# Layer 1's query-key scores of a hybrid encoder: three passes of rounded halves in two row tiles in place of native float32 products

## The chip, the cores and the metric

The kernel runs on one NeuronCore of one Trainium2 chip, as one launch. The metric is the device time of an execution in microseconds (us). The engines are TensorE (PE: matmuls; PEld: its weight loads, which overlap them), VectorE (DVE), ScalarE (ACT), GpSimdE (POOL) and SyncE (SP), each working through its own instructions in order and waiting on semaphores for the others.

## The reference

Two layers of a bidirectional encoder on x of 512 tokens by 1024 channels, all in float32. What a layer does, and of it the part that the change touches:

```python
h = modulate(rms_norm(x, norm1_g[l]), sh1, sc1)
z = h @ w_in[l]                      # split into za, zb, zq, zk, zv
# attention: 4 heads, 2 components of 64 dimensions each, 128 queries at a time
q = apply_rope(rms_norm(q, q_g), cos, sin) * (QK_HEAD_DIM ** -0.5)
k = apply_rope(rms_norm(k, k_g), cos, sin)
s = jnp.einsum("bqhcd,bkhcd->bhcqk", qb, k)
p = jax.nn.softmax(s, axis=-1)
w = p[:, :, 0] - lam * p[:, :, 1]
o = jnp.einsum("bhqk,bkhe->bqhe", w, v)
# beside it a 31-tap convolution and a gated 3-tap convolution, all three normed
x = x + g1 * (concat(ya, yb, yc) @ w_out[l])
x = x + g2 * swiglu(modulate(rms_norm(x, norm2_g[l]), sh2, sc2))
```

## The kernel before

Channels lie on the 128 partitions and the 512 tokens along the free axis. Every large product is made of three passes in the type float32r, which is float32 rounded to fewer bits: for each operand a rounded half ("hi") and a remainder ("lo") are kept, and hi·hi, hi·lo and lo·hi are summed in PSUM. `product` (L1294 to L1299) is one such triple for a chunk of 128 channels and 512 tokens. The weights arrive as a stream of units of 128 x 1024; ScalarE writes each unit's rounded half (`split_hi`, L539) and VectorE the remainder (`split_lo`, L842), into rings of four.

A layer runs as units on TensorE: the input projection for convolution and keys, for queries (four units), for values (four), then six units of the short convolution (the B units, `b_part`, each in four parts), which are dealt out among the attention's tiles; then W_out, the gate and up product and the down product.

After the projection the keys and queries are normed and rotated on VectorE (`qk_rotate`, L1021 to L1035) into `qk`, with tokens on the partitions. TensorE transposes them head by head: the keys (L1444) into PSUM banks 0 to 3, one bank for a head, ScalarE copies these to `k_t` (`copy_k_t`, L608), and then the queries (L1453) into the same four banks, once the copy of the key that lies there is done; ScalarE copies them to `q_t` (`copy_q_t`, L612). These copies hold 128 partitions: the first component of a head on partitions 0 to 63, the second on 64 to 127.

There are 16 attention tiles, a head by 128 queries each. For a tile TensorE makes `scores` (L1486), two native float32 products, one for each component, on 64 rows of the array each (two row tiles), into a pair of banks. VectorE takes the row maximum (`row_max`, L1040), ScalarE the two exponentials with their sums (`exps`, L621), VectorE the reciprocals (`row_inverse`, L1047), ScalarE scales the first component (`scale_p0`, L630), VectorE mixes in the second (`row_mix_in`, L1055), TensorE transposes the result (`weights_t`, L1499), ScalarE copies it out (`copy_w_t`, L639), and `attend` (L1511) multiplies by the values.

The order on each engine is written out by hand. On TensorE, tile `it` is: a part of a B unit, an attend step of an earlier head, `scores(it + 2)`, another part of the B unit, `weights_t(it)`. `scores(0)` and `scores(1)` stand behind the transposes of the queries and the B part 0, and B parts 1 to 3 behind them. On ScalarE: `copy_w_t(it - 1)`, `scale_p0(it)`, `exps(it + 1)`, then what else the tile has. On VectorE, between `qk_rotate` and the first `row_max` stand the remainders of three weight units and eight taps of the 31-tap convolution (`conv_a_taps`, L959), and in the tiles, behind `row_max(it + 1)` and `row_mix_in(it)`, more taps, the short convolution and a unit's remainder in every second tile. The buffers of the mixer lie over those of the feed-forward part; behind the mixer's there is a spare region of 16 KB a partition.

Of the kernel before, what the change touches and what calls it, by code (L numbers as in the profile page):

```python
# [7 lines left out]
F32 = mybir.dt.float32  # L8
F32R = mybir.dt.float32r
I32 = mybir.dt.int32  # L10
ALU = mybir.AluOpType
ACT = mybir.ActivationFunctionType
AX_X = mybir.AxisListType.X

P = 128
D = 1024
T = 512
# [9 lines left out]
HEADS = 4  # L27
DV = 128
DQ = 64
# [118 lines left out]
def encoder_kernel(nc, x_in, c_in, pos_in, freq_in, pcol_in, rows_in, ada_in, w_in, out):  # L148
    ctx = ExitStack()
    with ctx:  # L150
        top = [nc.sbuf_base]

        def place(name, shape, dt=F32, at=None):

            size = 4 * int(np.prod(shape[1:]))
            size += -size % 32
            if at is None:
                at = top[0]
                top[0] += size
            return nc.alloc_sbuf_tensor_at(name, shape, dt, offset=at), at + size  # L160
# [4 lines left out]
        def sem(name):  # L165
            return ctx.enter_context(nc.semaphore(name))
# [48 lines left out]
        at = gu_base  # L215
        ua, at = place("ua", [P, CC, T + 2 * PAD_A], at=at)
        uc, at = place("uc", [P, CC, T], at=at)
        hb, at = place("hb", [P, CC, T + 2 * PAD_B], at=at)
        yb, at = place("yb", [P, CC, T], at=at)
        rope_base = at  # L220
        tn, at = place("tn", [P, 2, T], at=at)
        tb, at = place("tb", [P, 2, T], at=at)
        ta, at = place("ta", [P, 2, T], at=at)
        prob, _ = place("prob", [P, PROBS, 2, T], at=rope_base)
        qk_base = at
        qk, at = place("qk", [P, 2, NT, T], at=at)
        w_t = [place(f"w_t{i}", [P, NT, T], at=qk_base + 4 * NT * T * i)[0] for i in range(2)]
        v, at = place("v", [P, NT, T], at=at)
        qt_base = at
        q_t, at = place("q_t", [P, HEADS, T], at=at)  # L230
        k_t, at = place("k_t", [P, HEADS, T], at=at)
        oc0, _ = place("oc0", [P, T], at=sq_base)
        oc1, at = place("oc1", [P, T], at=at)
        oc = [oc0, oc1]
        spare_base = at
        at += 4 * 4 * D
        c_row, _ = place("c_row", [1, D], at=spare_base)
        lam_prod, at = place("lam_prod", [P, 2 * L, DQ], at=at)
        assert at <= gu_end, "the mixer's buffers fit gu"


        sq0, _ = place("sq_first", [P, KC, T], at=h_lo_base)
        turns, at = place("turns", [P, NT, HALF, len(TERMS)], at=rope_base)
        whole, at = place("whole_turns", [P, NT, HALF, len(TERMS)], at=at)
        ang, at = place("ang", [P, 5, NT, HALF], at=at)
        ang_hi, at = place("ang_hi", [P, NT, HALF], F32R, at=at)
        assert at <= qk_base
        first_ring, at = place("ada_ring_first", [P, 8, D], at=qk_base)
        assert at <= qt_base + 4 * HEADS * T
        mid_a, _ = place("ada_ring_mid_a", [P, 4, D], at=spare_base)  # L250
        mid_b, _ = place("ada_ring_mid_b", [P, 4, D], at=qt_base)
        gu_ring, at = place("ada_ring_gu", [P, 4, D], at=gu_end - 4 * 4 * D)
        assert at <= gu_end and 4 * 4 * D == 4 * T * (FC - 2 * GU_MOD_STEPS)
        late_ring, at = place("ada_ring_late", [P, 8, D], at=h_base)
# [12 lines left out]
        ps = ctx.enter_context(nc.psum_tensor("ps", [P, 8, T], F32))  # L267
# [80 lines left out]
        s_qt = sem("q_t_ready")  # L348
        s_kt = sem("k_t_ready")

        s_scores = sem("scores_ready")
        s_max = sem("max_ready")
        s_exp = sem("exp_ready")
# [181 lines left out]
        def _(act):  # L535
# [69 lines left out]

            def copy_k_t(l, h):
                act.wait_ge(s_ktr, HEADS * l + h + 1)
                act.activation(k_t[:, h, :], ps[:, h, :], ACT.Copy).then_inc(s_kt, 1)  # L608

            def copy_q_t(l, h):  # L610
                act.wait_ge(s_qtr, HEADS * l + h + 1)
                act.activation(q_t[:, h, :], ps[:, h, :], ACT.Copy).then_inc(s_qt, 1)  # L612

            def exps(l, it):
                I = N_TILES * l + it
# [97 lines left out]
            for l in range(L):  # L713
# [45 lines left out]
                for h in range(HEADS):  # L759
                    copy_k_t(l, h)  # L760
# [75 lines left out]
        def _(dve):  # L836
# [172 lines left out]
            def qk_rotate(l, X, t):  # L1009
# [24 lines left out]
                dve.wait_ge(s_rot, 2 * E + 2)  # L1034
                dve.tensor_tensor(qk[:, X, t], ta[:, e % 2], tb[:, e % 2], ALU.add).then_inc(s_rope, 1)  # L1035

            def row_max(l, it):
                dve.wait_ge(s_scores, N_TILES * l + it + 1)
                b = 2 * (it % 2)
                dve.tensor_reduce(neg_max[:, it, :], ps[:, b:b + 2, :], AX_X, ALU.max,  # L1040
                                  negate=True).then_inc(s_max, 1)

            def row_inverse(l, it):

                I = N_TILES * l + it
                dve.wait_ge(s_exp, 2 * I + 2)
                dve.reciprocal(row_inv[:, it, :], row_sum[:, it, :]).then_inc(s_inv, 1)  # L1047
# [57 lines left out]
            for l in range(L):  # L1105
# [20 lines left out]
                for s in range(first, U_B):  # L1126
# [36 lines left out]
                    if l == 0 and s == U_V + 2:  # L1163
# [6 lines left out]
                                              ALU.mult).then_inc(s_lam, 1)  # L1170
                        dve.wait_ge(s_lam, 2 * L)

                row_max(l, 0)
                row_inverse(l, 0)
                for it in range(N_TILES):
# [110 lines left out]
        def _(pe):  # L1286
# [19 lines left out]
            h, gu = (h_hi, h_lo), (gu_hi, gu_lo)  # L1306
# [46 lines left out]
            def token_chunk(u, n, t, bank):  # L1353

                r = n % 2
                hs = [p[:, n, t * P:(t + 1) * P] for p in h]
                ws = [w[:, u % RING, r * T:(r + 1) * T] for w in (w_hi, w_lo)]
                pe.matmul(ps[:, bank, :], hs[0], ws[0], start=n == 0, stop=False)  # L1358
                pe.matmul(ps[:, bank, :], hs[0], ws[1], start=False, stop=False)  # L1359
                return pe.matmul(ps[:, bank, :], hs[1], ws[0], start=False, stop=n == KC - 1)  # L1360
# [30 lines left out]
            for b in range(2):  # L1391
                mm = pe.matmul(ps[:, b, :], ones[0:1, :], c_row[:, b * T:(b + 1) * T], start=True, stop=True)
            mm.then_inc(s_cps, 1)
            warm_up(N_WARM)
            for k in range(0, KC, 2):
                pe.wait_ge(s_pair, k // 2 + 1)
                mm = pe.matmul(ps[:, B_STAT, :], ones[:], sq0[:, k, :], start=k == 0, stop=k == KC - 2)
# [3 lines left out]
            for l in range(L):  # L1401
# [11 lines left out]
                for kk in range(N_Q):  # L1413
                    u = U + U_Q + kk
                    weights_split(u)
                    for t in range(NT):
# [6 lines left out]
                        for n in (2 * kk, 2 * kk + 1):  # L1423
                            mm = token_chunk(u, n, t, B_Q[t])
                    mm.then_inc(s_unit, 1)

                for kk in range(N_V):
                    u = U + U_V + kk
                    weights_split(u)
                    for t in range(NT):  # L1430
# [3 lines left out]
                        for n in (2 * kk, 2 * kk + 1):  # L1434
                            mm = token_chunk(u, n, t, B_KV[t])
# [13 lines left out]
                for hd in range(HEADS):  # L1449

                    pe.wait_ge(s_kt, HEADS * l + hd + 1)
                    for tt in range(NT):
                        tr = pe.transpose(ps[:, hd, tt * P:(tt + 1) * P], qk[:, 1, tt, hd * P:(hd + 1) * P], ident[:])  # L1453
                    tr.then_inc(s_qtr, 1)
# [20 lines left out]
                def scores(it):  # L1475
                    hd, qt = divmod(it, NT)
                    if it < 2:

                        pe.wait_ge(s_qt, HEADS * l + 2 * it + 2)
                        pe.wait_ge(s_kt, HEADS * (l + 1))  # L1480
                    else:

                        pe.wait_ge(s_exp, 2 * (N_TILES * l + it - 1))
                    for comp in range(2):
                        r = slice(DQ * comp, DQ * (comp + 1))
                        mm = pe.matmul(ps[:, 2 * (it % 2) + comp, :], q_t[r, hd, qt * P:(qt + 1) * P],  # L1486
                                       k_t[r, hd, :], start=True, stop=True)
                    mm.then_inc(s_scores, 1)
# [36 lines left out]
                for it in range(N_TILES):  # L1525
                    if 0 < it < 2 * N_B - 1:
                        b_part(2 * it + 2)
                    hd, kt = divmod(it - NT - 1, NT)
# [42 lines left out]
                with pe.Fori(0, 2) as i:  # L1571
                    for c in range(4):
# [3 lines left out]
                        for j, nb in enumerate(DOWN_BLOCKS):  # L1576
                            pe.wait_ge(s_gu, FC * l + f + nb)
                            unit(U + U_DOWN + 3 * c + j, B_DOWN + c % 2, gu, range(f, f + nb), i, 12,
                                 start=j == 0, stop=j == len(DOWN_BLOCKS) - 1)
# [83 lines left out]
```

## Time and profile before

| what | value |
|---|---|
| median of 3 runs | 1229.51 us (1228.2 to 1231.56) |
| the profiled execution's own time | 1227.94 us |
| its span, first to last instruction | 1226.1 us |
| mean granted TensorE clock, share of full speed | 0.986 |
| PE busy | 1185.7 us, 97% of the span |
| PE weight loads | 926.8 us, 76% |
| VectorE busy | 717.6 us, 59% |
| ScalarE busy | 481.1 us, 39% |
| GpSimdE busy | 104.5 us, 9% |
| layer 1's attention tiles | about 724 to 811 us of the span |

Matmuls are pipelined: a row's duration holds the way through the array, and the distance from one start to the next is what a matmul costs in a stream. A group of rows of one kind is merged into one line with its count.

### The profile page before, as it was taken

How to read it: one execution, taken by the hardware profiler on the slowest of the kernel's cores; microseconds unless marked ns; L12 is line 12 of the kernel's file. 1: busy time of each engine (PE TensorE's matmuls, PEld its weight loads, DVE VectorE, ACT ScalarE, POOL GpSimd, SP SyncE). 2: the span in 40 equal slices, each digit the busy share in tenths (PEclk: the TensorE clock that was granted, in tenths of full speed). 3: DMA queues.
4: the chain of work that ended last, by engine and by line, in shares of the span. 5: the costliest groups of instructions: out<-in, count | busy, mean ns of one | idle time of the engine just before them, and what ended most of it. 6: DMA issues, size and time to landing. Idle time of an engine off the chain costs nothing.

```text
span 1226.1 us, 14230 instructions
## 1 busy us (share of the span) xinstructions
PE 1185.7 (97%) x5090; PEld 926.8 (76%) x5090; DVE 717.6 (59%) x1022; ACT 481.1 (39%) x720; POOL 104.5 (9%) x177
## 2 busy tenths in 40 slices
PE   8999998979999999999989999889899999999998
PEld 5887545858888888888868876457788888888887
DVE  7889987876556433466656999746633333333331
ACT  5555777342332322322242356764422322322220
POOL 2411323101012000111000001100000000000000
PEclk9999999989999999999989999999999999999999
DMA  8686445646565232677313221103132232233322
GB/s 312 242 235 156 88 106 201 227 152 223 188 202 186 91 103 93 267 248 248 137 68 104 86 69 52 52 1 121 69 103 97 92 103 92 96 103 104 103 103 86
DMA packets 46345, 165.71 MB, mean 135 GB/s; under 512 B 5409, under 2 KB 5537, under 8 KB 46306
## 3 DMA queue, kind: packets, MB, share of 16 engines
q1 hardware_dynamic: 30386, 107.13, 25.9%
q0 software_dynamic: 15920, 58.07, 15.3%
q8 instruction: 23, 0.38, 0.1%
q14 instruction: 16, 0.13, 0.0%
HBM read 163.09 MB, written 2.10 MB: 135 GB/s over the span
## 4 chain that ended last, share of the span: by engine, by line
PE 78%; DVE 13%; ACT 3%; issue 3%; DMA 2%; SPq 0%; POOL 0%; DVEq 0%; ACTq 0%
PE ps L1297 21%; PE ps L1299 21%; PE ps L1298 21%; PE ps L1327 3%; DVE uc L959 2%; DVE w_lo L842 2%; PE ps L1511 2%; PE ps L1486 2%; PE ps L1331 2%; PE ps L1386 1%; DMA ada_ring_first<-ada 1%; DMA raw<-w_stream 1%; ACT prob L621 1%; DVE tn L1021 1%; DVE neg_max L1040 1%
## 5 line engine op out<-in xcount | busy, mean ns | idle before, releaser
L539 ACT ACTIVATE w_hi<-raw 128x1024 fp32r<-128x1024 f32 x196 | 207.8, 1060 | 570.6 <-PE ps L1299 494.7
L842 DVE TENSOR_TENSOR w_lo<-raw,w_hi 128x1024 fp32r<-128x1024 f32 x182 | 223.3, 1227 | 266.1 <-ACT w_hi L539 265.8
L1297 PE MATMUL ps<-h_hi,w_hi 128*128 128x512 f32 x848 | 334.5, 394 | 0.0
L1299 PE MATMUL ps<-h_lo,w_hi 128*128 128x512 f32 x848 | 330.4, 390 | 0.0
L1298 PE MATMUL ps<-h_hi,w_lo 128*128 128x512 f32 x848 | 330.2, 389 | 0.0
L1297 PEld LDWEIGHTS ps<-h_hi,w_hi 128*128 128x128 f32 x848 | 159.2, 188 | 48.3 <-issue 16.7
L1299 PEld LDWEIGHTS ps<-h_lo,w_hi 128*128 128x128 f32 x848 | 159.2, 188 | 33.2
L1298 PEld LDWEIGHTS ps<-h_hi,w_lo 128*128 128x128 f32 x848 | 159.3, 188 | 31.8
L1297 PE MATMUL ps<-gu_hi,w_hi 128*128 128x512 f32 x352 | 136.9, 389 | 0.0
L1298 PE MATMUL ps<-gu_hi,w_lo 128*128 128x512 f32 x352 | 136.9, 389 | 0.0
L1299 PE MATMUL ps<-gu_lo,w_hi 128*128 128x512 f32 x352 | 136.9, 389 | 0.0
L1245 DVE TENSOR_TENSOR work_b<-ps,work_a 128x512 f32<-128x512 f32 x44 | 30.4, 691 | 115.8 <-PE ps L1299 92.4
L959 DVE SCALAR_TENSOR_TENSOR uc<-ua,pcol,uc 128x512 f32<-128x512 f32 x120 | 83.9, 743 | 0.0
L1297 PEld LDWEIGHTS ps<-gu_hi,w_hi 128*128 128x128 f32 x352 | 66.1, 188 | 13.8
L1299 PEld LDWEIGHTS ps<-gu_lo,w_hi 128*128 128x128 f32 x352 | 66.1, 188 | 13.7
L1298 PEld LDWEIGHTS ps<-gu_hi,w_lo 128*128 128x128 f32 x352 | 66.1, 188 | 13.6
L1358 PE MATMUL ps<-w_hi,h_hi 128*128 128x512 f32 x192 | 75.1, 391 | 0.1
L1360 PE MATMUL ps<-w_hi,h_lo 128*128 128x512 f32 x192 | 74.7, 389 | 0.0
L1359 PE MATMUL ps<-w_lo,h_hi 128*128 128x512 f32 x192 | 74.7, 389 | 0.0
L621 ACT ACTIVATE prob<-ps,neg_max 128x512 f32<-128x512 f32 x64 | 43.5, 685 | 34.9 <-DVE neg_max L1040 34.9
L1089 DVE SCALAR_TENSOR_TENSOR xT<-ps,mod,xT 128x512 f32<-128x512 f32 x32 | 24.0, 750 | 52.9 <-PE ps L1299 50.4
L444 POOL TENSOR_SCALAR row_mix<-row_inv,neg_lam 128x1 f32<-128x1 f32 x32 | 26.3, 823 | 223.1 <-DVE row_inv L1047 223.1
(171 smaller groups left out, 1301.0 us busy)
## 6 DMA issues: line engine op xcount, KB each, us to landing
raw<-w_stream SPq DMA_DIRECT2D x196, 512.0 KB, 3.3
ada_ring_gu<-ada POOLq DMA_DIRECT2D x28, 512.0 KB, 4.1
ada_ring_late<-ada POOLq DMA_DIRECT2D x28, 512.0 KB, 4.7
ada_ring_first<-ada POOLq DMA_DIRECT2D x16, 512.0 KB, 5.4
w_lo<-w_stream POOLq DMA_DIRECT2D x14, 512.0 KB, 7.7
ada_ring_mid_a<-ada POOLq DMA_DIRECT2D x12, 512.0 KB, 6.2
ada_ring_mid_b<-ada POOLq DMA_DIRECT2D x12, 512.0 KB, 4.6
xT<-x_t SPq DMA_DIRECT2D x4, 512.0 KB, 5.6
```

The source lines that it names most:

```text
L539: act.activation(w_hi[:, u % RING, :], raw[:, u % RAW, :], ACT.Copy).then_inc(s_whi, 1)
L621: act.activation(prob[:, it % PROBS, comp, :], ps[:, 2 * (it % 2) + comp, :], ACT.Exp, bias=neg_max[:, it, comp:comp + 1], accum_out=row_s ...
L842: dve.tensor_tensor(w_lo[:, u % RING, :], raw[:, u % RAW, :], w_hi[:, u % RING, :].bitcast(F32), ALU.subtract).then_inc(s_wlo, 1)
L959: dve.scalar_tensor_tensor(uc[:, c, :], ua[:, c, j:j + T], w, uc[:, c, :], ALU.mult, ALU.add).then_inc(s_tap, 1)
L1245: dve.tensor_tensor(wb[:, f, :], ps[:, j, :], wa[:, f, :], ALU.mult).then_inc(s_pr, 1)
L1297: pe.matmul(dst, whi, rhs[0][:, n, :], start=start, stop=False)
L1298: pe.matmul(dst, wlo, rhs[0][:, n, :], start=False, stop=False)
L1299: return pe.matmul(dst, whi, rhs[1][:, n, :], start=False, stop=stop)
L1327: pe.matmul(ps[:, bank, :], wp[:, u % RING, n * P:(n + 1) * P], h_hi[:, n, :], start=b == 0 and wp is w_hi, stop=False)
L1358: pe.matmul(ps[:, bank, :], hs[0], ws[0], start=n == 0, stop=False)
L1359: pe.matmul(ps[:, bank, :], hs[0], ws[1], start=False, stop=False)
L1360: return pe.matmul(ps[:, bank, :], hs[1], ws[0], start=False, stop=n == KC - 1)
```

## The change

In layer 1 alone, the copies of the transposed keys and queries are written as float32r (rounded) into the places where `k_t` and `q_t` lay. VectorE gets eight new subtractions, four `k_low` and four `q_low`, which read the transposed head from its PSUM bank, subtract the rounded copy, and write the remainder to two new buffers in the spare region. They stand in VectorE's order between the last tap ahead of the tiles and the first `row_max`. On TensorE the transposes of query head `hd` wait for `k_low(hd)` too, since they overwrite the bank that it reads, and `scores(0)` and `scores(1)` wait for the remainders. `scores` in layer 1 is six float32r matmuls of 64 rows by 512 columns, the two components taking turns: hi·hi, lo·hi, hi·lo of each. Layer 0 keeps its native products.

```diff
--- before.py
+++ after.py
@@ -229,12 +229,16 @@
         qt_base = at
         q_t, at = place("q_t", [P, HEADS, T], at=at)
         k_t, at = place("k_t", [P, HEADS, T], at=at)
+        q_r, _ = place("q_t_hi", [P, HEADS, T], F32R, at=qt_base)
+        k_r, _ = place("k_t_hi", [P, HEADS, T], F32R, at=qt_base + 4 * HEADS * T)
         oc0, _ = place("oc0", [P, T], at=sq_base)
         oc1, at = place("oc1", [P, T], at=at)
         oc = [oc0, oc1]
         spare_base = at
         at += 4 * 4 * D
         c_row, _ = place("c_row", [1, D], at=spare_base)
+        q_lo, k_lo_at = place("q_t_lo", [P, HEADS, T], F32R, at=spare_base)
+        k_lo, _ = place("k_t_lo", [P, HEADS, T], F32R, at=k_lo_at)
         lam_prod, at = place("lam_prod", [P, 2 * L, DQ], at=at)
         assert at <= gu_end, "the mixer's buffers fit gu"
 
@@ -348,6 +352,8 @@
         s_qt = sem("q_t_ready")
         s_kt = sem("k_t_ready")
 
+        s_klo = sem("k_t_lo_ready")
+        s_qlo = sem("q_t_lo_ready")
         s_scores = sem("scores_ready")
         s_max = sem("max_ready")
         s_exp = sem("exp_ready")
@@ -605,11 +611,11 @@
 
             def copy_k_t(l, h):
                 act.wait_ge(s_ktr, HEADS * l + h + 1)
-                act.activation(k_t[:, h, :], ps[:, h, :], ACT.Copy).then_inc(s_kt, 1)
+                act.activation((k_r if l else k_t)[:, h, :], ps[:, h, :], ACT.Copy).then_inc(s_kt, 1)
 
             def copy_q_t(l, h):
                 act.wait_ge(s_qtr, HEADS * l + h + 1)
-                act.activation(q_t[:, h, :], ps[:, h, :], ACT.Copy).then_inc(s_qt, 1)
+                act.activation((q_r if l else q_t)[:, h, :], ps[:, h, :], ACT.Copy).then_inc(s_qt, 1)
 
             def exps(l, it):
                 I = N_TILES * l + it
@@ -1033,6 +1039,18 @@
                 dve.wait_ge(s_cos, E + 1)
                 dve.wait_ge(s_rot, 2 * E + 2)
                 dve.tensor_tensor(qk[:, X, t], ta[:, e % 2], tb[:, e % 2], ALU.add).then_inc(s_rope, 1)
+
+            def k_low(h):
+
+                dve.wait_ge(s_kt, HEADS + h + 1)
+                dve.tensor_tensor(k_lo[:, h, :], ps[:, h, :], k_r[:, h, :].bitcast(F32),
+                                  ALU.subtract).then_inc(s_klo, 1)
+
+            def q_low(h):
+
+                dve.wait_ge(s_qt, HEADS + h + 1)
+                dve.tensor_tensor(q_lo[:, h, :], ps[:, h, :], q_r[:, h, :].bitcast(F32),
+                                  ALU.subtract).then_inc(s_qlo, 1)
 
             def row_max(l, it):
                 dve.wait_ge(s_scores, N_TILES * l + it + 1)
@@ -1170,6 +1188,11 @@
                                               ALU.mult).then_inc(s_lam, 1)
                         dve.wait_ge(s_lam, 2 * L)
 
+                if l:
+                    for h in range(HEADS):
+                        k_low(h)
+                    for h in range(HEADS):
+                        q_low(h)
                 row_max(l, 0)
                 row_inverse(l, 0)
                 for it in range(N_TILES):
@@ -1449,6 +1472,8 @@
                 for hd in range(HEADS):
 
                     pe.wait_ge(s_kt, HEADS * l + hd + 1)
+                    if l:
+                        pe.wait_ge(s_klo, hd + 1)
                     for tt in range(NT):
                         tr = pe.transpose(ps[:, hd, tt * P:(tt + 1) * P], qk[:, 1, tt, hd * P:(hd + 1) * P], ident[:])
                     tr.then_inc(s_qtr, 1)
@@ -1478,9 +1503,21 @@
 
                         pe.wait_ge(s_qt, HEADS * l + 2 * it + 2)
                         pe.wait_ge(s_kt, HEADS * (l + 1))
+                        if l:
+                            pe.wait_ge(s_klo, HEADS)
+                            pe.wait_ge(s_qlo, 2 * it + 2)
                     else:
 
                         pe.wait_ge(s_exp, 2 * (N_TILES * l + it - 1))
+                    if l:
+                        cols = slice(qt * P, (qt + 1) * P)
+                        for i, (q, k) in enumerate(((q_r, k_r), (q_lo, k_r), (q_r, k_lo))):
+                            for comp in range(2):
+                                r = slice(DQ * comp, DQ * (comp + 1))
+                                mm = pe.matmul(ps[:, 2 * (it % 2) + comp, :], q[r, hd, cols], k[r, hd, :],
+                                               start=i == 0, stop=i == 2)
+                        mm.then_inc(s_scores, 1)
+                        return
                     for comp in range(2):
                         r = slice(DQ * comp, DQ * (comp + 1))
                         mm = pe.matmul(ps[:, 2 * (it % 2) + comp, :], q_t[r, hd, qt * P:(qt + 1) * P],
```

## Rows read from the trace of the kernel before

**Rows 1.** Window: length, PE, PEld, DVE, ACT, POOL busy us; granted clock; DMA.

```profile
740.00:780.00 40.00, 39.99 (x167) 24.32 (x167) 36.95 (x56) 27.09 (x58) 5.01 (x8) 1.00 0.17 59
```

**Rows 2.** Timeline of PE at the tiles' start: start, length, engine, line, operation.

```profile
720.56 1.91 PE L1453 MATMUL ps<-ident,qk 128*128 128x128 f32 x16
722.22 0.48 PE L1297 MATMUL ps<-h_hi,w_hi 128*128 128x512 f32 x1
...
723.79 1.99 PE L1486 MATMUL ps<-k_t,q_t 64*128 64x512 f32 x8
725.71 0.50 PE L1297 MATMUL ps<-h_hi,w_hi 128*128 128x512 f32 x1
```

**Rows 3.** Timeline of DVE in the same stretch.

```profile
724.22 1.41 DVE L959 SCALAR_TENSOR_TENSOR uc<-ua,pcol,uc 128x512 f32<-128x512 f32 x2
725.55 1.22 DVE L1040 TENSOR_REDUCE neg_max<-ps 128x2 f32<-128x1024 f32 x1
728.29 0.17 DVE L1047 RECIPROCAL row_inv<-row_sum 128x2 f32<-128x2 f32 x1 [1.51 <-ACT prob L621]
```

**Rows 4.** Timeline of DVE: a 128x512 two-operand step out of PSUM, and its successor.

```profile
745.51 0.68 DVE L967 TENSOR_TENSOR hb<-ps,yb 128x512 f32<-128x512 f32 x1
746.11 1.21 DVE L842 TENSOR_TENSOR w_lo<-raw,w_hi 128x1024 fp32r<-128x1024 f32 x1
```

**Rows 5.** Timeline of ACT: the four copies of the queries.

```profile
722.20 2.05 ACT L612 ACTIVATE q_t<-ps 128x512 f32<-128x512 f32 x4
```

**Rows 6.** Timeline of PE about scores(4).

```profile
736.95 0.39 PE L1298 MATMUL ps<-h_hi,w_lo 128*128 128x512 f32 x1
737.17 0.40 PE L1299 MATMUL ps<-h_lo,w_hi 128*128 128x512 f32 x1
737.50 1.13 PE L1486 MATMUL ps<-k_t,q_t 64*128 64x512 f32 x4
738.56 0.50 PE L1297 MATMUL ps<-h_hi,w_hi 128*128 128x512 f32 x1
738.89 0.39 PE L1298 MATMUL ps<-h_hi,w_lo 128*128 128x512 f32 x1
```

**Rows 7.** Line L1486 alone at scores(4): durations min/median/max, first and last start.

```profile
L1486 PEld LDWEIGHTS ps<-k_t,q_t x4: 183/184/186, 737.5 to 737.6; 64*128 64x128 f32 x4
L1486 PE MATMUL ps<-k_t,q_t x4: 589/641/693, 737.5 to 738.0; 64*128 64x512 f32 x4
```

**Rows 8.** Timeline: the mixes and transposes of tiles 4 and 10, and copy and scaling behind.

```profile
748.38 0.74 DVE L1055 SCALAR_TENSOR_TENSOR prob<-prob,row_mix 128x512 f32<-128x512 f32 x1
749.17 0.66 PE L1499 MATMUL ps<-ident,prob 128*128 128x128 f32 x4
...
782.17 0.60 PE L1499 MATMUL ps<-ident,prob 128*128 128x128 f32 x4
782.81 0.60 ACT L639 ACTIVATE w_t<-ps 128x512 f32<-128x512 f32 x1 [1.73 <-PE ps L1499]
784.05 0.75 DVE L1055 SCALAR_TENSOR_TENSOR prob<-prob,row_mix 128x512 f32<-128x512 f32 x1 [1.62 <-ACT prob L630]
```

**Rows 9.** Timeline of PE: what follows an idle stretch in layer 1's tiles.

```profile
790.44 1.04 PE L1499 MATMUL ps<-ident,prob 128*128 128x128 f32 x4 [3.01 <-DVE prob L1055]
```

**Rows 10.** Windows, columns as in the first group: behind two idle stretches of PE.

```profile
793.00:794.00 1.00, 1.00 (x3) 0.54 (x2) 0.00 (x0) 1.00 (x3) 0.00 (x0) 0.51 0.00 0
794.00:795.00 1.00, 1.00 (x3) 0.44 (x3) 0.04 (x1) 1.00 (x3) 0.00 (x0) 1.00 0.00 0
...
633.00:634.00 1.00, 1.00 (x4) 0.78 (x4) 1.00 (x2) 0.27 (x2) 0.00 (x0) 0.72 0.00 0
```

**Rows 11.** Timeline of PE at the start of layer 1, behind an idle stretch.

```profile
627.94 0.77 PE L1343 MATMUL ps<-h_hi,w_hi 128*128 128x512 f32 x1 [3.13 <-ACT h_hi L577]
628.50 0.63 PE L1344 MATMUL ps<-h_hi,w_lo 128*128 128x512 f32 x1
628.93 0.63 PE L1343 MATMUL ps<-h_hi,w_hi 128*128 128x512 f32 x1
```

## The prediction

> **What bounds the kernel now.** I read the windows first. In layer 1's tiles from 740 to 780 us TensorE is busy for 39.99 of 40 us and VectorE for 36.95, at full granted clock [rows 1]: both are nearly full, and the change takes work from the one and gives work to the other. So the question is which of them sets the pace where. Next I read the timelines at the start of the tiles. TensorE goes from the key and query transposes through the B part 0 and the first two scores to the next B part, from 720.56 to 725.71, with no idle entry [rows 2]. VectorE works off its last taps (724.22) and takes the first row maximum at 725.55, the moment it gets to it [rows 3]; the scores were there by then. Until tile 10 TensorE lags a little behind VectorE. For tile 4 the weights are mixed at 748.38 + 0.74 = 749.12 and the transposes start at 749.17, so here the two meet. For tile 10 it is TensorE that is late: its transposes start at 782.17, ScalarE had waited 1.73 us for them, and VectorE 1.62 us for ScalarE [rows 8]. From there to W_out the chain runs through VectorE and ScalarE; a delay that reaches it reaches the end, because W_out, gate and up and down are a closed stream of TensorE.
>
> **The saving in scores, per tile.** A float32r matmul in a stream costs 0.22 to 0.23 us from start to start (736.95 to 737.17). The native scores(4) run from 737.50 to 738.56, 1.06 us, and the matmul behind is followed by the next at 0.33 instead of 0.23, as is the one ahead of scores: a switch costs some 0.1 us on either side, and I leave it as it is [rows 6]. The line's own view gives four matmuls with two starts, 737.5 and 738.0: the two components run at the same time in the two row tiles, in two rounds of some 0.47 us, with 0.12 left over [rows 7]. The change makes it three rounds of one float32r pass. If the two row tiles run together as the native ones do, a round is 0.23 us at the least and, with the 0.04 that the native round has over its 0.43 (two passes of 0.213), 0.27 at the most; I take 0.25. Then scores cost 3 x 0.25 + 0.12 = 0.87, a saving of 0.19 us; the bounds are 0.81 and 0.93, a saving of 0.25 or 0.13. I round up to 0.2 a tile since the switch may shrink with the type unchanged. Sixteen tiles would be 3.2 us, but only a part of them counts, as follows.
>
> **The new wait, which is the larger term.** `k_low(0)` stands behind the taps in VectorE's order, so it can't start before 725.55 [rows 3], though the key's transposes and copies were done about 7 us earlier. The query transposes, at 720.56 before [rows 2], wait for it. What is queued behind that wait on TensorE: the B part 0, the scores, all tiles. A `k_low` is a two-operand step of 128x512 out of PSUM: 0.68 us, 0.60 from start to start [rows 4]. So `k_low` 0 to 3 end at 726.24, 726.84, 727.45 and 728.05, and TensorE, its values done by about 720.6, idles for some 5.5 us.
>
> After idle stretches the clock was low. Behind 3.01 us of idle the four transposes at 790.44 took 1.04 instead of 0.60 us [rows 8, 9], and the granted clock was about half until 794.0 [rows 10], 3.6 us after work resumed. Behind 3.13 us at the start of layer 1, matmuls came 0.43 us apart instead of 0.23 [rows 11], and the clock was back only in the 633 to 634 window, 5.6 us after the work resumed [rows 10]. Both levels are those of 1.2 and 2.4 GHz. An idle of 5.5 us will do the same, so I take the low clock for the transposes and the B part 0. The Trainium skill, "TensorE: Matmul & The Clock Gate", section "HAM oscillation — how this bites in real kernels", warns of exactly such gaps between bursts; the trace agrees, with the two stretches above.
>
> The chain then: a head's four transposes take 4 x 0.213 = 0.85 at the low clock (the 1.04 less the way out of the array), so from 726.3 four heads end at 729.7. ScalarE copies at 0.5 to 0.6 each [rows 5], the last done at 730.5; `q_low` 0 to 3 end at about 728.8, 729.5, 730.3 and 731.2. The B part 0, six matmuls, takes 6 x 0.43 = 2.6 instead of about 1.5, so it ends at 732.3. scores(0), waiting on `q_low(1)` only, run from 732.35 to 733.2, and the row maximum can start at about 733.25 instead of 725.55: **VectorE is 7.7 us late.** Bounds: if the clock is back after 3.6 us, 1.0 us less (6.7); if it stays low through scores(0) too, 0.8 more (8.5); if it never falls, the transposes follow `k_low` to 728.55, the B part ends at 730.05, the row maximum starts at 731.2: 5.65 late. The eight subtractions themselves (8 x 0.60 = 4.8 us of VectorE) lie inside this delay.
>
> **What is given back.** scores(1) end about 0.85 us behind scores(0), so TensorE comes to the B part 1 about 8.1 us late (725.71 before). It gains 0.2 a tile and meets VectorE again at tile 4, where there was no slack; from there VectorE's 7.7 is what counts. Of the scores behind that, 7 to 12 are ahead of the transposes of tile 10: 6 x 0.2 = 1.2 us, all of it within the 1.73 us that ScalarE waited there [rows 8]. So 1.2 us comes back, 1.7 at most. Scores 13 to 15 have slack, and save nothing. VectorE's other short waits in the tiles are on ScalarE, which is delayed with it, so I let them give nothing back; if they did, they hold 40 - 36.95 = 3 us in the 40 us [rows 1].
>
> **The rest at no cost.** The copies in float32r are the same size on the same engine; the remainders of weight units move with VectorE, and the rings are two units ahead; no DMA is moved or added.
>
> **Sum.** 7.7 - 1.2 = 6.5 us on the profiled execution's 1227.94: 1234.4. The median of the runs shown is 1229.51, 1.57 above the profiled one; on the median the forecast is **1236.0 us**. Bounds of this case: 5.0 (6.7 - 1.7) to 8.0 (8.5 with little given back), 1234.5 to 1237.5.
>
> **Rivals.**
> 1. *Not slower than can be measured: the clock stays up or the delay is soaked up.* Were TensorE not slowed after the gap, VectorE would be 5.65 late, and 1.2 to 1.7 would come back: 4.0 to 4.5. If in addition VectorE's waits in the tiles (3 us) give back 1 us or more, the sum is about 3: 1232.5. Against it: two of two rows behind gaps of 3 us show the low clock. It decides from a delay under 3.7 us. Chance 0.15.
> 2. *The two row tiles do not run together in float32r.* Then scores cost 6 x 0.227 + 0.12 = 1.48, 0.42 more a tile than native, and TensorE, not VectorE, is behind throughout. scores(0) make the delay 8.3, scores(1) another 1.0, scores 2 to 12 eleven times 0.42 = 4.6, so tile 10's transposes are 13.9 late: about 1243.4. For it: no row shows float32r in row tiles; against it: native ones run in pairs [rows 7]. Chance 0.08.
> 3. *They run together, but a row tile's next weight load is not hidden under its own matmul.* Transposes of 128 columns follow each other at about 0.11 us (four from 782.17, the last ending at 782.77 [rows 8]), which I take as the bound of a load: a round 0.23 + 0.11 = 0.34, scores 1.13, 0.07 more than native. The delay is 8.0, TensorE another 0.7, plus 11 x 0.07 = 0.8: 9.4, or 1238.9. Chance 0.10. The Trainium skill ("TensorE: Matmul & The Clock Gate", section "The mechanism" of its part on packing) says that loads overlap matmuls in flight only where the row group differs, which would speak for this rival; the loads of scores(4) start at 737.5 and 737.6, the second pair while the first pair's matmuls run on the same rows [rows 7], which speaks against it.
> 4. *Faster.* It would need the query transposes not to wait for the taps; the order on VectorE is fixed, and the saving in scores, 0.25 x 16 = 4 us at the very best, is under even the shortest delay. Chance 0.02.
>
> **How the numbers follow.** The forecast's case has 0.65. The range of 80% takes in its bounds, rival 3 and the upper part of rival 1: 1232.0 to 1240.0 us; rival 2, the faster case and the lower part of rival 1 are left out. About 0.3% (3.7 us) is what a measurement of this kernel can tell from no change. Faster by more: 0.02. Within: rival 1 and a little of the forecast's case where more is given back, 0.17. Slower: 0.81.
>
> **What would show it.** In the profile after: an idle of about 5.5 us ahead of the query transposes, released by `k_low` on VectorE; granted clock 0.5 behind it for 3 to 6 us; the first row maximum about 7.7 us later against the start of the query transposes of before; scores from start to the next matmul 0.87 us with pairs of starts; the wait of ScalarE for tile 10's transposes shrunk from 1.73 to about 0.5. I am wrong if the gap is there and the first row maximum is less than 5.5 us late, if scores cost over 1.06, or if the distance from the first row maximum to the first W_out matmul shrinks by more than 2 us.

## The result, and the profile after

The changed kernel takes 1234.25 us (median of 13 runs, 1232.68 to 1235.7), the kernel before 1227.94 us beside it (13 runs, 1224.82 to 1231.56): a ratio of 1.0054, with a 95% interval of 1.0044 to 1.0063. That is 6.6 us slower (5.4 to 7.7). The two medians by themselves differ by 6.3 us: here and below, the us by which a kernel is slower or faster are the ratio applied to the time of the kernel before, and the difference of the medians is up to 1.1 us away from that. The forecast was 6.5 us slower; its absolute figure, 1236.0, is 1.75 us too high, mostly because the first three runs of the kernel before, on which it stood, had a median of 1229.51, 1.57 above that of all 13.

The spans of the two profiled executions differ by 5.7 us (1231.8 against 1226.1), but the key transposes of layer 1 start at 712.64 us after and at 716.02 before, although nothing ahead of them was changed. So the stretches are measured from that start. "To tile 13's row maximum" begins at the first row maximum, and "to first W_out matmul" at tile 13's. Three profiles of each kernel, all in us:

| | key transposes to first row maximum | to tile 13's row maximum | to first W_out matmul | sum |
|---|---|---|---|---|
| before, three profiles | 9.53, 9.53, 9.53 | 62.96, 62.94, 62.96 | 17.79, 18.99, 18.36 | 90.28, 91.46, 90.85 |
| after, three profiles | 17.42, 16.02, 16.97 | 61.91, 61.89, 61.87 | 18.97, 18.11, 18.71 | 98.30, 96.02, 97.55 |

The means of the sums are 90.9 and 97.3: 6.4 us, inside the measured 5.4 to 7.7. The first stretch loses 7.3 us on the mean, the second gives back 1.06, and the third is 0.2 longer on the mean (18.38 and 18.60), while it moves by up to 1.2 us between executions of one kernel. From the first W_out matmul to the end of the span it takes 419.8, 420.9 and 420.7 us before and 420.9, 420.5 and 420.8 after, which adds 0.3.

The gap, in TensorE's timeline after (start, length, engine, line, operation, count, and in brackets the idle time ahead and who ended it):

```profile
716.94 0.39 PE L1383 MATMUL ps<-w_hi,h_lo 128*128 128x512 f32 x1
723.00 3.64 PE L1478 MATMUL ps<-ident,qk 128*128 128x128 f32 x16 [5.68 <-DVE k_t_lo L1046]
726.30 0.78 PE L1320 MATMUL ps<-h_hi,w_hi 128*128 128x512 f32 x1
726.87 0.63 PE L1321 MATMUL ps<-h_hi,w_lo 128*128 128x512 f32 x1
727.30 0.63 PE L1322 MATMUL ps<-h_lo,w_hi 128*128 128x512 f32 x1
```

TensorE idles 5.68 us ahead of the query transposes, which follow the last value product at once in [rows 2]. The 16 transposes take 3.64 us for 1.91 there, and the B part's matmuls stand 0.43 us apart. VectorE in the same stretch:

```profile
720.85 1.41 DVE L965 SCALAR_TENSOR_TENSOR uc<-ua,pcol,uc 128x512 f32<-128x512 f32 x2
722.18 2.47 DVE L1046 TENSOR_TENSOR k_t_lo<-ps,k_t_hi 128x512 fp32r<-128x512 f32 x4
724.76 0.69 DVE L1052 TENSOR_TENSOR q_t_lo<-ps,q_t_hi 128x512 fp32r<-128x512 f32 x1
727.32 0.69 DVE L1052 TENSOR_TENSOR q_t_lo<-ps,q_t_hi 128x512 fp32r<-128x512 f32 x1 [0.16 <-ACT q_t_hi L618]
730.06 1.23 DVE L1058 TENSOR_REDUCE neg_max<-ps 128x2 f32<-128x1024 f32 x1 [2.06 <-PE ps L1517]
```

Where the first row maximum stood behind the last taps in [rows 3], now the four key subtractions stand, and the row maximum waits another 2.06 us for the scores. Four windows of this stretch (length, busy time of PE, PEld, DVE, ACT and POOL, granted clock, DMA share, GB/s):

```profile
721.00:722.00 1.00, 0.00 (x0) 0.00 (x0) 1.00 (x2) 0.00 (x0) 0.00 (x0) 1.00 0.00 0
723.00:724.00 1.00, 1.00 (x5) 1.00 (x6) 1.00 (x3) 0.00 (x0) 0.00 (x0) 0.50 0.63 254
727.00:728.00 1.00, 1.00 (x4) 0.81 (x3) 0.84 (x2) 0.28 (x1) 0.00 (x0) 0.50 0.00 0
729.00:730.00 1.00, 1.00 (x9) 0.81 (x10) 0.00 (x0) 0.00 (x0) 0.00 (x0) 1.00 0.00 0
```

VectorE is busy alone, then the granted clock is half (1.2 GHz) until the 729 window. The new scores, and the transposes of tile 10 with what they release, answering to [rows 6] and [rows 8]:

```profile
742.11 0.50 PE L1517 MATMUL ps<-k_t_hi,q_t_hi 64*128 64x512 f32 x2
742.45 0.39 PE L1517 MATMUL ps<-k_t_hi,q_t_lo 64*128 64x512 f32 x2
742.68 0.40 PE L1517 MATMUL ps<-k_t_lo,q_t_hi 64*128 64x512 f32 x2
743.01 0.50 PE L1320 MATMUL ps<-h_hi,w_hi 128*128 128x512 f32 x1
...
785.62 0.60 PE L1536 MATMUL ps<-ident,prob 128*128 128x128 f32 x4
786.26 0.60 ACT L645 ACTIVATE w_t<-ps 128x512 f32<-128x512 f32 x1 [0.72 <-PE ps L1536]
787.50 0.75 DVE L1073 SCALAR_TENSOR_TENSOR prob<-prob,row_mix 128x512 f32<-128x512 f32 x1 [0.56 <-ACT prob L636]
```

Three pairs of starts, and 0.90 us from the first to the next matmul, for 1.06 before. ScalarE waits 0.72 us for the transposes of tile 10, for 1.73, and VectorE 0.56 for 1.62: that is the 1.06 us given back (1.62 - 0.56).

### The profile page after: what moved, and what is told of

It is laid out like the page before. It is cut to its first block, busy times and chain, and to the rows that moved or that the text cites. A ratio compares the mean times of both kernels' runs of the same rounds, so it can differ in the third digit from the quotient of the medians.

```text
span 1231.8 us, 14307 instructions
## 1 busy us (share of the span) xinstructions
PE 1185.9 (96%) x5122; PEld 932.8 (76%) x5122; DVE 722.4 (59%) x1030; ACT 481.4 (39%) x720; POOL 105.4 (9%) x177
## 4 chain that ended last, share of the span: by engine, by line
PE 80%; DVE 13%; ACT 4%; issue 3%; DMA 0%; DVEq 0%; ACTq 0%
PE ps L1320 21%; PE ps L1322 21%; PE ps L1321 21%; PE ps L1350 3%; DVE uc L965 3%; DVE w_lo L848 2%; PE ps L1548 2%; PE ps L1354 2%; DVE neg_max L1058 1%; ACT prob L627 1%; PE ps L1366 1%; PE ps L1367 1%; PE ps L1371 1%; PE ps L1381 1%; PE ps L1383 1%
```

## The experiments

Each ratio is against the kernel before, with its 95% interval. "Sum" is the way from the key transposes to the first W_out matmul in the experiment's profile (before 90.3 to 91.5, after 96.0 to 98.3).

**The wait without the passes.** Layer 1's scores stay native and read unrounded copies; the remainders are made and not used.

```diff
-                    if l:
-                        cols = slice(qt * P, (qt + 1) * P)
-                        for i, (q, k) in enumerate(((q_r, k_r), (q_lo, k_r), (q_r, k_lo))):
...
-                        return
```

> The eight subtractions and all their waits as in the changed kernel, but layer 1's scores stay native float32 (from unrounded copies; the remainders are computed and not used). My theory (the early wait costs, the passes give a little back): the idle of some 5.7 us ahead of the query transposes and the low clock behind it stay, the first row maximum is about 8 us late, and what the changed kernel got back at tile 10 (ScalarE's wait there went from 1.73 to 0.72 us) is not given back: 1 to 1.2 us slower than the changed kernel, so some 7.5 to 8 us over the kernel before, a ratio of 1.0062. Rival (the passes themselves are what costs, by row tiles or accumulation): this kernel is clearly faster than the changed one, ratio under 1.003.

Measured: 1.0062 (1.0046 to 1.0078), 7.6 us over the kernel before; sum 98.5 with only 3.4 us of low clock in the gap. ScalarE at tile 10, and VectorE behind it:

```profile
787.14 0.60 ACT L645 ACTIVATE w_t<-ps 128x512 f32<-128x512 f32 x1 [1.73 <-PE ps L1527]
788.38 0.75 DVE L1073 SCALAR_TENSOR_TENSOR prob<-prob,row_mix 128x512 f32<-128x512 f32 x1 [2.02 <-ACT prob L636]
```

Nothing is given back: the wait of 1.73 us is that of [rows 8]. From the first to tile 13's row maximum it takes 63.35 us for 61.91, so the passes save the changed kernel 1.44 us here. That is 0.4 more than they save against the kernel before, since VectorE's wait at tile 10 is 2.02 us here for 1.62 there; where these 0.4 come from is open. The subtractions and their waits hold the whole loss, as my theory has it; the rival that the passes cost something falls. That this kernel is slower than the changed one is shown by the stretch, not by the two ratios, whose intervals overlap.

**The passes without the wait.** Three passes of the rounded halves, without subtractions and their waits.

```diff
-                        for i, (q, k) in enumerate(((q_r, k_r), (q_lo, k_r), (q_r, k_lo))):
+                        for i, (q, k) in enumerate(((q_r, k_r), (q_r, k_r), (q_r, k_r))):
```

> Three float32r passes in the two row tiles as in the changed kernel, but all three take the rounded halves, and there are no subtractions and no waits for them. It leaves out the remainders, so the scores are three times the rounded product. My theory: 0.16 us less a tile on TensorE (scores 0.90 instead of 1.06), of which only what ScalarE waited for TensorE at tile 10 counts: 1.0 to 1.7 us faster than the kernel before, ratio 0.9988. Rival (TensorE sets the pace throughout, so all 16 tiles count): 2.6 us faster, 0.9979. Rival (float32r in row tiles costs): slower than before.

Measured: 0.9974 (0.9963 to 0.9986), 3.2 us faster (1.7 to 4.5), more than the 1.0 to 1.7 expected. ScalarE at tile 10:

```profile
779.25 0.60 ACT L645 ACTIVATE w_t<-ps 128x512 f32<-128x512 f32 x1 [0.72 <-PE ps L1526]
```

The same 0.72 as after, and 61.89 us from the first row maximum to tile 13's: 1.07 saved, as the theory has it. The time by itself speaks for the first rival: its 0.9979 lies inside the interval, and the theory's 0.9988 just outside. The stretch speaks against it, since the twelve scores in it at 0.16 us each would save 1.9 us if TensorE set the pace in all tiles. The sum is 89.3, 1.6 below the mean of before, and the way from W_out to the end is 419.9 us, 0.6 below; together 2.1 us, inside the measured 1.7 to 4.5. So the tiles answer as expected, and the half of these 2.1 us that lies behind tile 13 is of the size by which executions of one kernel differ there. Whether the passes have a part in it stays open.

**The gap filled.** 24 matmuls of 128x512 into a bank that is overwritten later, between the values and the query transposes.

```diff
+                if l:
+                    weights_split(U + U_B)
+                    pe.wait_ge(s_v, NT * l + 1)
+                    for i in range(24):
+                        pe.matmul(ps[:, B_KV[0], :], w_hi[:, (U + U_B) % RING, 0:P], h_hi[:, i % KC, :],
+                                  start=True, stop=True)
```

> The changed kernel with 24 matmuls of 128x512 float32r, whose results are overwritten later, between the last value product and the query transposes: they fill the idle 5.7 us (24 x 0.227 = 5.45) and end just before the transposes may start. If the low clock behind the gap costs 2.2 us, as the accounting says (first row maximum 7.9 us late against 5.65 with the clock up), the first row maximum comes about 2.2 us earlier and the kernel is 2 us faster than the changed one: ratio 1.0036. If the clock plays no part (all is VectorE's order), the time is that of the changed kernel, 1.0054.

Measured: 1.0024 (1.0015 to 1.0034), 2.9 us over the kernel before. TensorE and VectorE at the gap:

```profile
718.83 5.60 PE L1476 MATMUL ps<-h_hi,w_hi 128*128 128x512 f32 x24
724.68 2.42 PE L1484 MATMUL ps<-ident,qk 128*128 128x128 f32 x16 [0.24 <-DVE k_t_lo L1046]
726.86 0.48 PE L1320 MATMUL ps<-h_hi,w_hi 128*128 128x512 f32 x1
...
729.45 1.22 DVE L1058 TENSOR_REDUCE neg_max<-ps 128x2 f32<-128x1024 f32 x1 [0.73 <-PE ps L1523]
```

The transposes start when `k_low` lets them, 0.24 us behind the filler, and take 2.42 us for 3.64; the granted clock is 1.00 in all windows from 633 to 792 us. The first row maximum is 15.14 us behind the key transposes, 5.61 late; the forecast's bound for a clock that stays up was 5.65. So the low clock is a real part of the delay: 1.7 us (7.3 - 5.6) of the 7.3 that the three profiles after have on the mean. The rival, by which the time would be the changed kernel's 1.0054, falls. The loss in time is 2.9 us for the changed kernel's 6.6, so 3.7 us less, more than this; the sum (95.7) is only 1.6 below the changed kernel's mean, and where the rest went was not found.

**The subtractions earlier in VectorE's order.** Same work, other place.

```diff
+                    if l and s == U_V + 1:
+                        for h in range(HEADS):
+                            k_low(h)
+                    if l and s == U_V + 2:
+                        for h in range(HEADS):
+                            q_low(h)
                     if s in TAPS_UNIT[l]:
                         conv_a_taps(l, TAPS_UNIT[l][s])
```

> The changed kernel with the four key subtractions moved ahead of the last eight taps, and the four query subtractions behind the first two of them and one weight unit's remainder, ahead of the last six taps. Same work. My theory: the wait of the query transposes goes (no idle ahead of them, clock stays up there), and scores(0) start about as before; but the last taps now stand between the subtractions and the first row maximum, which is 4.8 us late (8 x 0.60), and TensorE idles about 3 us ahead of scores(2) instead. With 1 us back at tile 10: 4 us slower than the kernel before, ratio 1.0033, 2.5 us faster than the changed one. Rival (the cost is the subtractions' own length and not their place in the order): no different from the changed kernel, 1.0054.

Measured: 1.0033 (1.002 to 1.0046), 4.1 us over the kernel before, 2.5 less than the changed one; sum 95.2. VectorE:

```profile
717.48 2.48 DVE L1046 TENSOR_TENSOR k_t_lo<-ps,k_t_hi 128x512 fp32r<-128x512 f32 x4
...
722.33 2.48 DVE L1052 TENSOR_TENSOR q_t_lo<-ps,q_t_hi 128x512 fp32r<-128x512 f32 x4
724.72 2.73 DVE L965 SCALAR_TENSOR_TENSOR uc<-ua,pcol,uc 128x512 f32<-128x512 f32 x4
727.37 1.22 DVE L848 TENSOR_TENSOR w_lo<-raw,w_hi 128x1024 fp32r<-128x1024 f32 x1
728.51 1.41 DVE L965 SCALAR_TENSOR_TENSOR uc<-ua,pcol,uc 128x512 f32<-128x512 f32 x2
729.84 1.21 DVE L1058 TENSOR_REDUCE neg_max<-ps 128x2 f32<-128x1024 f32 x1
```

The first row maximum is 4.80 us late, which is the eight subtractions at 0.60 and nothing else. TensorE's idle moved: 0.42 and 0.23 us ahead of the first two scores, 2.37 ahead of the third, and here the clock stayed up until tile 12 (1.00 in the windows from 729 to 738). The rival's 1.0054 is outside the interval. Place alone is worth some 2.5 us (the intervals of the two kernels just touch, but the first stretch takes 14.33 us for 16.02 to 17.42), and the work still costs.

**VectorE's order rewritten around them.** The first row maximum right behind the query subtractions, three taps in VectorE's wait for the first exponentials, three taps and a remainder later, and the remainder of tile 11 moved as in the next experiment.

```diff
-13: 2, 14: 4, 15: 2})
+13: 2, 14: 3})
...
+                        for h in range(HEADS):
+                            q_low(h)
+                        row_max(l, 0)
...
+                    if it == 13:
+                        split_lo(U + U_B + N_B - 1 + RING)
```

> The changed kernel's computation with VectorE's order rewritten in layer 1: key subtractions ahead of the last eight taps, query subtractions behind two of them and one weight unit's remainder, the first row maximum right behind them, three taps while ScalarE makes the first exponentials, the remainder of the next weight unit at the end of tile 0, three taps later (tiles 9, 10 and 12), and the remainder of tile 11 moved behind the row maximum of tile 13's turn. My theory (place in VectorE's order was the cost; the 4.8 us of subtractions are paid only where VectorE has no idle time): first row maximum within 0.5 us of before, 1.5 us of the subtractions go into the wait for the first exponentials, 2 to 2.6 us stay in the tiles, 1 to 1.6 us come back at tile 11, 1.1 us by the moved remainder: within 0.5 us of the kernel before, ratio 1.000 (0.999 to 1.001). Rival (VectorE's work is paid in full wherever it stands): 4.8 - 1.1 - 1.1 = 2.6 us slower, 1.002.

Measured: 1.0001 (0.999 to 1.0011), as my theory has it; the rival's 1.002 is outside, but see the next experiment, which changes what the rival would give. The first row maximum is 0.28 us earlier than before, the stretch to tile 13's takes 63.28 us (1.37 over after, with five taps of 0.66 us more in it), the sum is 90.3:

```profile
724.74 1.22 DVE L1058 TENSOR_REDUCE neg_max<-ps 128x2 f32<-128x1024 f32 x1
725.88 2.06 DVE L965 SCALAR_TENSOR_TENSOR uc<-ua,pcol,uc 128x512 f32<-128x512 f32 x3
727.86 0.16 DVE L1065 RECIPROCAL row_inv<-row_sum 128x2 f32<-128x2 f32 x1
```

The wait of 1.51 us ahead of the first reciprocals [rows 3] is gone, filled with taps. TensorE behind tile 12 here, and a window:

```profile
789.95 1.09 PE L1546 MATMUL ps<-ident,prob 128*128 128x128 f32 x4 [2.37 <-DVE prob L1073]
...
790.00:791.00 1.00, 1.00 (x4) 0.63 (x4) 0.75 (x3) 1.00 (x5) 0.00 (x0) 0.51 0.00 0
```

So here the clock fell behind an idle of 2.37 us, the length behind which it stayed up in the experiment before. The passes can be had at the time of the kernel before. But part of this edit, the moved remainder, has nothing to do with the passes, and what it gives has to be taken off.

**One remainder moved in the kernel before.** The last part of that edit alone, on the kernel before. The lines stand in the loop of both layers, but in layer 0 VectorE does not write this remainder (a DMA does), so only layer 1 changes.

```diff
                     if it + 1 < N_TILES:
                         row_max(l, it + 1)
+                    if it == 13:
+                        split_lo(U + U_B + N_B - 1 + RING)
                     row_mix_in(l, it)
...
-                    if it % 2 and it < 2 * N_B:
+                    if it % 2 and it < 2 * N_B - 1:
```

> The kernel before, with one thing moved in VectorE's order in layer 1: the remainder of the weight unit at tile 11 (1.13 us, ahead of the row maximum of tile 13, for which ScalarE waits 2.43 us) goes behind the row maximum of tile 14, where VectorE idles for 2.37 us. If the stretch behind tile 10 hangs on VectorE and ScalarE, as I take it, 1.1 us faster than before, ratio 0.9991; if on TensorE, no change.

Measured: 0.9977 (0.9966 to 0.9988), 2.8 us faster (the medians, 1224.44 and 1227.76, differ by 3.3), and faster than both kernels. The stretch to tile 13's row maximum is 1.13 us shorter (61.83), as expected. TensorE behind tile 12, and a window there:

```profile
786.11 0.66 PE L1501 MATMUL ps<-ident,prob 128*128 128x128 f32 x4 [1.88 <-DVE prob L1055]
...
787.00:788.00 1.00, 0.43 (x1) 0.30 (x2) 1.00 (x2) 1.00 (x3) 0.27 (x1) 1.00 0.00 0
```

The idle ahead of tile 12's transposes is 1.88 us for 3.01 [rows 9], and the granted clock stays full in the windows of 1 us from 783 to 790, and on to 857, where before it fell. That may be why more than 1.1 us was gained, on the average over executions: in the one profile the sum (89.2) is 1.7 below the mean of before, and the way from W_out to the end (419.8 us) 0.7 below.

This sets the experiment before in another light. Its rival counted 1.1 us for the moved remainder; with the measured 2.8 the rival gives 4.8 - 1.1 - 2.8 = 0.9 us, or 1.0007, which is inside that kernel's interval, so the time does not rule it out. The profiles do, one of each: both take 17.79 us from tile 13's row maximum to W_out, and the reordered kernel's sum is 1.17 us longer than this one's, where subtractions paid in full would be 4.8 - 1.1 = 3.7. In time the reordered kernel is 2.9 us slower than this one (some 1 to 5 by the two intervals). So against a kernel before with the same remainder moved, the passes still cost.

**The passes in another order.** The three of the first component, then the three of the second.

```diff
-                        for i, (q, k) in enumerate(((q_r, k_r), (q_lo, k_r), (q_r, k_lo))):
-                            for comp in range(2):
+                        for comp in range(2):
+                            for i, (q, k) in enumerate(((q_r, k_r), (q_lo, k_r), (q_r, k_lo))):
```

> The changed kernel with the six score matmuls in another order: the three passes of the first component, then the three of the second, in place of taking turns. Same matmuls. If two row tiles overlap only where neighbours in the order lie in different tiles, only the third pass of the first and the first of the second overlap: 5 x 0.227 + 0.12 = 1.26 us in place of 0.90, no pairs of starts but one; then TensorE is late again at tile 10 (0.36 x 12, less the 0.41 us of slack at tile 4): 3 to 4.5 us slower than the changed kernel, ratio 1.008 to 1.009. If the engine pairs them whatever their order, the scores stay at 0.90 and the time at 1.0054. If the row tiles do not overlap at all in either, both are 1.48 and no different.

Measured: 1.0044 (1.003 to 1.0059), no different from the changed kernel. The scores:

```profile
743.97 0.50 PE L1517 MATMUL ps<-k_t_hi,q_t_hi 64*128 64x512 f32 x2
744.30 0.40 PE L1517 MATMUL ps<-k_t_hi,q_t_lo 64*128 64x512 f32 x2
744.54 0.40 PE L1517 MATMUL ps<-k_t_lo,q_t_hi 64*128 64x512 f32 x2
744.87 0.50 PE L1320 MATMUL ps<-h_hi,w_hi 128*128 128x512 f32 x1
```

Again pairs, and 0.90 us. In the built program the order is as written, one component after the other, so the fourth matmul in order runs beside the first. Whether TensorE pairs them, or what lies between the built program and the chip, the trace does not tell. The Trainium skill, "TensorE: Matmul & The Clock Gate", section "The mechanism", says of row tiles that matmuls start and end strictly in program order and only weight loads are pulled ahead; if TensorE gets them as built, these scores would by that take 1.26 us, an estimate from the 0.227 us of a pass, and the trace does not agree.

**Both kernels profiled again.**

> The changed kernel itself, a second profile. In its first profile the granted clock was low for 6.8 us in the gap ahead of the query transposes, again for 6.8 us behind tile 12, and for 6.8 us behind the norm ahead of gate and up, where the kernel before shows 3.4 us in the last two. If these lengths belong to the change, they are the same again; if they differ from one execution to the next, at least one of the three is 3.4 us here, and the 2.3 us that they cost in the profiles are no part of the change.

> The changed kernel, a third profile. The delay of the first row maximum against the key transposes of layer 1 was 7.9 us in the first profile, with 6.8 us of low clock in the gap, and 6.5 us in the second, with 3.4 us. If the clock alone makes the difference, this one is one of the two values, by the length of its low stretch.

> The kernel before itself, a second profile. If the length of a stretch at low clock changes from one execution to the next in this kernel too, the stretch behind tile 12 or the one behind the norm (both 3.4 us in the first profile) is 6.8 us here, or the one at the start of layer 1 (6.8) is 3.4. If the kernel fixes them, all three are as before.

> The kernel before, a third profile, to the same end: the row maximum of tile 0 comes 9.53 us behind the start of the key transposes whatever the clock does elsewhere, since no idle stretch of TensorE lies between; the way from there to W_out is 80.75 us with 3.4 us of low clock behind tile 12 and about 1.1 us longer with 6.8.

The stretches are in the table above. In the second profile after, VectorE and a window of the gap:

```profile
727.75 1.29 DVE L1052 TENSOR_TENSOR q_t_lo<-ps,q_t_hi 128x512 fp32r<-128x512 f32 x2 [0.16 <-ACT q_t_hi L618]
729.95 1.22 DVE L1058 TENSOR_REDUCE neg_max<-ps 128x2 f32<-128x1024 f32 x1 [0.91 <-PE ps L1517]
...
727.00:728.00 1.00, 1.00 (x8) 0.92 (x7) 0.84 (x2) 0.87 (x2) 0.00 (x0) 0.91 0.00 0
```

The clock was back by the 727 window; the low stretch was 3.4 us, and the row maximum waited 0.91 us for the scores instead of 2.06. In the third it was 6.8 us long again, and the delay 7.44: so two executions with 6.8 us differ by 0.45 (against the transposes' start, the clock fell about 1 us earlier in the third), and my expectation of just two values was too simple. In the second profile of the kernel before, behind tile 12:

```profile
789.08 1.12 PE L1499 MATMUL ps<-ident,prob 128*128 128x128 f32 x4 [3.01 <-DVE prob L1055]
792.38 3.59 PE L1386 MATMUL ps<-work_a,ones 128*128 128x512 f32 x4
```

The idle is the 3.01 us of [rows 9], but the low clock lasted 6.8 us for 3.4, the statistics' four matmuls took 3.59 us, and the way to W_out 18.99 for 17.79. The third had 3.4 us there and 18.36. So the length of the low clock behind tile 12 changes from one execution to the next in both kernels (3.4, 6.8 and 3.4 us before; 6.8, 3.4 and 6.8 after), and what the first profile after shows more of it there is no part of the change. Behind the norm it is 3.4, 6.8 and 6.8 us before and 6.8 in all three after; the kernel before shows both lengths there, and three profiles do not tell whether the change makes the longer one more frequent.

## Why the prediction was right, point by point

- *The early wait and the idle.* 5.5 us forecast, 5.68 measured, released by `k_low` in all three profiles. The step that found it was to read at what time VectorE comes to the new instruction (725.55) and not how long the instruction is.
- *The clock.* Forecast low for the transposes and the B part. So it was in the first profile, the one that is 7.89 late; in the third it came back in the middle of the B part, and in the second at the end of the transposes. The forecast put 2.05 us on it (7.7 - 5.65). The filled gap shows the size: 5.61 late with the clock up, 6.5 to 7.9 without, 1.7 us on the mean.
- *The first row maximum.* Forecast 7.7 late (6.7 to 8.5); measured 7.89, 6.49 and 7.44. The mean is 7.3, and the lowest is 0.2 under my lower bound.
- *Scores.* Forecast 0.87 (0.81 to 0.93), and 0.2 saved a tile; measured 0.90, and 0.16. The term is 0.04 too large. The row tiles run together, so rival 2 falls, and no load shows between the passes, which come 0.23 us apart, so rival 3 does too. (Its terms add up to 9.5 us, not 9.4.)
- *What comes back.* Forecast 1.2, at tile 10, by ScalarE's wait; measured 1.06. VectorE and TensorE met at tile 4, as read: TensorE waits 0.41 us there in the profile after.
- *VectorE's short waits in the tiles.* Forecast to give nothing back; its row maxima from tile 0 to 12 come within 0.02 us of the distances of before.
- *The sum.* 6.5 forecast, 6.6 measured. Each term is within 0.5 us of the mean of the profiles, so the mechanism holds, but that the sum is within 0.1 is luck: the delay was 0.4 too large and what comes back 0.1 too large, and behind tile 13, where nothing was forecast, the profiles after are 0.2 us longer to W_out and 0.3 from there to the end.
- Not foreseen: executions differ in how long the clock stays low, so that a single profile could have shown any loss from 4.6 to 8.0 us (sums of after and before paired in their order give 8.0, 4.6 and 6.7).

## What to carry to other kernels

When a step is moved to cheaper passes that need a new operand, look first where the engine that makes it comes to it in its own order, and who stands behind it: here a saving of 0.16 us a tile, of which 1 us counts, was bought with a wait of 5.7 us that only the place in the queue caused. Another place took the wait away and gave back 2.5 of the 6.6 us; the 4.8 us of new work on VectorE still had to find idle time there, and against a kernel with the same other move, the rewritten order still lost 1.2 us in the profiles and 2.9 in time. An idle stretch of TensorE costs more than its length if the clock falls behind it; moving 1 us of VectorE's work from ahead of such a gap into one of its idle times gained 2.8 us. Test such a move on the old kernel too, or its gain is put down to the new one. And where parts of the kernel vary by microseconds between executions, compare stretches between two marks, from several profiles, and not spans.

## What the runs showed of the hardware

- Matmuls on two row tiles ran in pairs even where three of one tile stand ahead of the other tile's first in the built program: 0.90 us for six either way.
- The same kernel, behind the same 3.01 us of idle, ran at 1.2 GHz for 3.4 us in one execution and for 6.8 us in another. The way from tile 13's row maximum to W_out moved with it by up to 1.2 us (17.79 and 18.99). In a third execution it was 3.4 us again, but fell 2.1 us behind the end of the idle, and the way was 18.36.
- Behind tile 12, an idle of 1.88 us (one remainder moved) was not followed by a low clock; those of 3.0 and 3.2 us were in every profile, and the 5.7 us one ahead of the query transposes too. An idle of 2.37 us is between: ahead of scores(2) (subtractions earlier) the clock stayed up, behind tile 12 (order rewritten) it fell for 3.4 us.
